# Four token-major projection blocks, first token halves shared between two engines, and a new start and end in a one-core transformer kernel

## The chip, the core and the metric

The kernel runs on one core of a Trainium2 chip. The core has a matrix engine (PE, with its weight load PEld), a vector engine (DVE), a scalar engine (ACT), GpSimd (POOL) and SyncE (SP), which here issues transfers. Data lie in SBUF, 128 partitions wide; PE writes to PSUM, whose banks hold 128 x 512 fp32 values. The metric is the device time of one execution in microseconds.

## The reference

The input is x, 256 tokens by 2048 features, with a memory of 256 rows. Two layers of one model (a pooling layer and a layer of compressed, selected and windowed attention, each with memory attention) are followed by a block of another: differential, stick-breaking and chunk-band attention side by side, an output projection, and a gated feed-forward part with a causal convolution, then a last norm. Cut to the lines that the change bears on:

```python
h = rmsnorm_2(x, attn_norm[l])
qkv = jnp.einsum('bsd,de->bse', h, w_qkv[l])
q_a, k_a, v_a, q_b, k_b, v_b, q_c, k_c, v_c = split_columns(qkv)
y_b = stick_breaking_attention(q_b, k_b, v_b, sb_norm[l])
y_c = chunk_band_attention(q_c, k_c, v_c, rel_bias[l], ch_norm[l])
...
x = x + jnp.einsum('bsf,fd->bsd', jax.nn.silu(g) * u, w_down[l])
return rmsnorm_2(x, final_norm)
```

In the program q_c, k_c, v_c are called qc, kcc, vcc, and q_b, k_b, v_b are qb, kb, vb; each is 512 wide, with eight heads of 64.

## The kernel before, in words

All weights pass through the core once, as 691 units of at most 128 x 1024 fp32 (512 KB), in the order of a plan. SP asks for a unit into one of four stage buffers `s_stage`. ACT copies it, rounded, into the high part of one of three buffers `s_w` (L1214), DVE subtracts that from the original and writes the low part (L1855), and PE multiplies high by high, high by low and low by high. The two steps are called the split. A buffer of `s_w` comes free when PE has finished the unit three before.

Each engine's program is written out by hand as one list. Its beat is the unit: `nxt` on ACT and DVE first gives every attached piece of side work one tick, then splits the next unit; on PE the tick comes after a unit's matmuls. `later(n, ...)` attaches work n ticks on. Engines meet by semaphores, and each list is worked off in order, so an instruction that waits holds what stands behind it.

A projection is done in one of two ways. Weight-stationary (`tile`, L586 and L587; `group`, L627 and L630): the weights are PE's stationary side, a unit is eight pairs of a matmul of 512 columns (the high and the low tokens) and one of 256, and the output has features on partitions and tokens in the columns. DVE then adds the two halves of the bank (L1900) and scales (L1907, L1909). Token-major (`pair`, L653 to L655): the tokens are stationary, a unit is twelve matmuls of 512 columns, and the output has tokens on partitions, one bank for each half of the 256 tokens. In the last unit of eight the first token half is finished first. DVE moves the first half out (L1922), ACT the second (L1244), with the row norm's factor. Only two banks, psg0 and psg1, serve all of this before the feed-forward part; they are taken in turn, and a first matmul into a bank waits until its last content is out.

The blocks of the feed-forward part are token-major with turned weights: ACT moves both halves to `s_ev` (L1611), and DVE transposes 32 x 32 blocks in four ticks of four instructions (`turn`, L2389), after which features lie on partitions again. They alternate between two pairs of banks.

The middle's order is qc, kcc, vcc, qb, kb, vb, all from the normalised second block's input `s_ry`. Side work there: the scaling of X by the final gain of the first model (L2306), and from the end of vcc on the chunk-band attention, four pairs of heads, six ticks apart: scores on PE (L978, L979), bias and maxima on DVE (L2324, L2325, L2047, L2048), exponentials on ACT (L1522), and the finish of a head (L2315, L2332).

At the start the memory's 256 rows come in pieces, are split with their gain (L1226 on ACT, L1873 on DVE) into `s_rh`, and the first units, of memory keys, go four tiles abreast over two column blocks of 128 features per unit. The first unit comes on ACT's queue in two halves (L1271, L1964). The squares for the memory's row norm are taken by ACT from a second copy (L1291), in bursts of four.

At the end, the last down-projection block leaves its last three units' second token half to the end; then for each token half come an addition (L2580), squares (L1652), a sum (L2584), logarithm and exponential (L1827, L1829), three refinements (L2588 to L2592), the scaling of four blocks of 512 on DVE and ACT (L2596, L2599, L1662), and four stores of 256 KB (L2957).

## Time and profile before

| | |
|---|---|
| median of 3 runs | 2006.98 us (2006.02 to 2007.39) |
| profiled execution | 2005.24 us, span 2003.4 us |
| PE busy | 1987.2 us, 99% of the span |
| DVE, ACT, POOL busy | 1499.9, 1065.5, 400.8 us |
| mean granted clock of PE | 0.999 |
| moved by the transfers | 374.80 MB, mean 187 GB/s |

A profile's times are those of one execution. A matmul's row gives its start and a duration that includes the pipeline, so the pace of PE is read from start to start, and durations of neighbours overlap. In brackets at the end of a row stands how long the engine was idle before it, and which engine, tile and line released it. DVE's next instruction may likewise start about 0.1 us before the end given for the last one.

### The profile page before, as it was taken

How to read it: one execution, taken by the hardware profiler on the slowest of the kernel's cores; microseconds unless marked ns; L12 is line 12 of the kernel's file. 1: busy time of each engine (PE TensorE's matmuls, PEld its weight loads, DVE VectorE, ACT ScalarE, POOL GpSimd, SP SyncE). 2: the span in 40 equal slices, each digit the busy share in tenths (PEclk: the TensorE clock that was granted, in tenths of full speed). 3: DMA queues.
4: the chain of work that ended last, by engine and by line, in shares of the span. 5: the costliest groups of instructions: out<-in, count | busy, mean ns of one | idle time of the engine just before them, and what ended most of it. 6: DMA issues, size and time to landing. Idle time of an engine off the chain costs nothing.

```text
span 2003.4 us, 27138 instructions
## 1 busy us (share of the span) xinstructions
PE 1987.2 (99%) x10380; PEld 1696.5 (85%) x10380; DVE 1499.9 (75%) x2180; ACT 1065.5 (53%) x1619; POOL 400.8 (20%) x379
## 2 busy tenths in 40 slices
PE   8999999999999999999999999999999999999998
PEld 7888988888888888888888888888888888888886
DVE  6776778788798666877656678688899545989954
ACT  6654544467534554654555555455555444555544
POOL 0014544300000444420222235200000100000120
PEclk9999999999999999999999999999999999999999
DMA  9664666567655334556444445655655655555564
GB/s 341 226 192 150 192 187 198 190 210 238 221 172 169 126 116 137 186 204 196 161 159 157 148 157 190 206 184 185 199 189 192 203 191 187 194 195 190 191 206 150
DMA packets 103795, 374.80 MB, mean 187 GB/s; under 512 B 11729, under 2 KB 13169, under 8 KB 103153
## 3 DMA queue, kind: packets, MB, share of 16 engines
q1 hardware_dynamic: 103376, 372.54, 56.8%
q8 instruction: 82, 1.34, 0.3%
q10 hardware_dynamic: 288, 0.52, 0.1%
q14 instruction: 49, 0.39, 0.1%
HBM read 370.92 MB, written 2.10 MB: 186 GB/s over the span
## 4 chain that ended last, share of the span: by engine, by line
PE 98%; DVE 1%; DMA 0%; ACT 0%; issue 0%; SPq 0%; ACTq 0%
PE psg L586 27%; PE psg L587 14%; PE psg L653 7%; PE psg L654 7%; PE psg L655 7%; PE pss L653 4%; PE pss L654 4%; PE pss L655 4%; PE pst L683 2%; PE pss L683 2%; PE pss L685 2%; PE pss L684 2%; PE pst L685 2%; PE pst L684 2%; PE psg L627 1%; PE pst L627 1%
## 5 line engine op out<-in xcount | busy, mean ns | idle before, releaser
L1855 DVE TENSOR_TENSOR s_w<-s_stage,s_w 128x1024 fp32r<-128x1024 f32 (+2 forms) x690 | 855.6, 1242 | 314.7 <-ACT s_w L1214 310.5
L1214 ACT ACTIVATE s_w<-s_stage 128x1024 fp32r<-128x1024 f32 (+2 forms) x690 | 725.5, 1053 | 667.0 <-PE psg L587 313.2
L586 PE MATMUL psg<-s_ry,s_w 128*128 128x512 f32 x1216 | 429.4, 394 | 0.2 <-DVE s_w L1855 0.2
L586 PE MATMUL psg<-s_rh,s_w 128*128 128x512 f32 x1216 | 427.6, 394 | 0.3 <-DVE s_w L1855 0.3
L587 PE MATMUL psg<-s_rh,s_w 128*128 128x256 f32 x1216 | 342.7, 282 | 0.0
L587 PE MATMUL psg<-s_ry,s_w 128*128 128x256 f32 x1216 | 342.6, 282 | 0.0
L586 PEld LDWEIGHTS psg<-s_ry,s_w 128*128 128x128 f32 x1216 | 228.3, 188 | 51.3 <-issue 4.1
L586 PEld LDWEIGHTS psg<-s_rh,s_w 128*128 128x128 f32 x1216 | 228.3, 188 | 48.9 <-issue 1.0
L587 PEld LDWEIGHTS psg<-s_rh,s_w 128*128 128x128 f32 x1216 | 229.8, 189 | 0.6
L587 PEld LDWEIGHTS psg<-s_ry,s_w 128*128 128x128 f32 x1216 | 229.8, 189 | 0.2
L653 PE MATMUL psg<-s_w,s_ry 128*128 128x512 f32 x512 | 201.2, 393 | 0.0
L655 PE MATMUL psg<-s_w,s_ry 128*128 128x512 f32 x512 | 199.4, 389 | 0.0
L654 PE MATMUL psg<-s_w,s_ry 128*128 128x512 f32 x512 | 199.4, 389 | 0.0
L2782 POOL TENSOR_TENSOR s_hid<-s_hh,s_hid 128x256 fp32r<-128x256 f32 x44 | 51.0, 1160 | 584.1 <-ACT s_hid L1637 584.1
L653 PE MATMUL pss<-s_w,s_ry 128*128 128x512 f32 x352 | 137.4, 390 | 0.0
L655 PE MATMUL pss<-s_w,s_ry 128*128 128x512 f32 x352 | 137.0, 389 | 0.0
L654 PE MATMUL pss<-s_w,s_ry 128*128 128x512 f32 x352 | 136.9, 389 | 0.0
L653 PEld LDWEIGHTS psg<-s_w,s_ry 128*128 128x128 f32 x512 | 96.1, 188 | 21.2 <-issue 0.8
L655 PEld LDWEIGHTS psg<-s_w,s_ry 128*128 128x128 f32 x512 | 96.1, 188 | 20.4
L654 PEld LDWEIGHTS psg<-s_w,s_ry 128*128 128x128 f32 x512 | 96.2, 188 | 19.2
L2650 POOL TENSOR_SCALAR s_bsc<-s_bsc,s_stat 128x256 f32<-128x256 f32 (+1 forms) x56 | 45.8, 836 | 184.7 <-DVE s_stat L2289 173.5
L2389 DVE STREAM_TRANSPOSE s_gg<-s_ev 32x256 f32<-32x256 f32 x176 | 76.7, 436 | 2.8
(424 smaller groups left out, 2973.9 us busy)
## 6 DMA issues: line engine op xcount, KB each, us to landing
s_stage<-in_wo SPq DMA_DIRECT2D x96, 512.0 KB, 3.5
s_stage<-in_wg SPq DMA_DIRECT2D x88, 512.0 KB, 3.3
s_stage<-in_wu SPq DMA_DIRECT2D x88, 512.0 KB, 3.3
s_stage<-in_wd SPq DMA_DIRECT2D x88, 512.0 KB, 3.4
s_stage<-in_ain SPq DMA_DIRECT2D x64, 512.0 KB, 3.7
s_stage<-in_wkv SPq DMA_DIRECT2D x32, 512.0 KB, 3.4
s_stage<-in_bq SPq DMA_DIRECT2D x24, 512.0 KB, 3.4
s_stage<-in_bzq SPq DMA_DIRECT2D x24, 512.0 KB, 3.2
```

Source lines behind the costliest of these rows:

```text
L586: e.matmul(o, M.WH[:, r, ws], xx, start=begin, stop=False)
L587: m = e.matmul(o[:, T:2 * T], M.WL[:, r, ws], xh, start=False, stop=end)
L653: e.matmul(o[:, :], xh[:, ts], M.WH[:, r, ws], start=(k == 0), stop=False)
L654: e.matmul(o[:, :], xh[:, ts], M.WL[:, r, ws], start=False, stop=False)
L655: m = e.matmul(o[:, :], xl[:, ts], M.WH[:, r, ws], start=False, stop=(k == 15))
L683: e.matmul(o, xh[:, ts], M.WH[:, r, ws], start=(k == 0), stop=False)
L684: e.matmul(o, xh[:, ts], M.WL[:, r, ws], start=False, stop=False)
L685: m = e.matmul(o, xl[:, ts], M.WH[:, r, ws], start=False, stop=(k == nk - 1))
L1214: e.activation(M.weights(c, 0, n, shift), M.staged(c, n), ACT.Copy).then_inc(S["wh"], 1)
L1855: e.tensor_tensor(M.weights(c, 1, n, shift), M.staged(c, n), M.weights(c, 0, n, shift), ALU.subtract).then_inc(S["wl"], 1)
L2389: x = e.transpose(dst[32 * r:32 * r + 32, :, :].rearrange("p c (t q i) -> p q t c i", t=2, q=4)[:, q, :, :, :], M.EV[32 * q:32 * q + 32, r ...
L2782: e.tensor_tensor(M.HID[:, 1, i, :], M.HH[j % 2][:, :], M.HID[:, 0, i, :].bitcast(F32), ALU.subtract).then_inc(S["hidl"], 1)
```

## The change

It has three parts.

Start: eleven matmuls of 128 columns on the constant tile `s_one` are issued by PE before its first unit. The second unit is asked for in two halves, ahead of memory pieces 2 and 3, and is split in halves. The first unit's matmuls are issued with the four tiles' high products first, then the low ones. Memory pieces 4 to 7 come in two transfers, the vector of constants later, and the squares of the memory's rows in bursts of two.

Middle: qc, kcc, qb and kb become token-major blocks with turned weights. ACT moves both token halves of qc and the second one of the three others into `s_ev2` (shown as `s_ev`); DVE moves the first half of kcc, qb and kb, with `first_half`, which stands in its list behind the split of the second unit after the block. Four turns follow in the ticks of the next block. The chunk-band and stick-breaking scores wait for the turns. The scaling of X begins 14 ticks later.

End: the second token half of the last three units is done in two halves of 256 columns, the second of them in a bank of its own; the sums of three of the four blocks' squares are taken ahead, the fourth enters through the logarithm's bias; DVE, ACT and POOL share the scaling; each token half is stored in two transfers of 512 KB.

Some semaphores of the constants' transfers are merged. The diff, cut to its core:

```diff
--- before.py
+++ after.py
-MEMP = ((0, 1), (1, 2), (2, 4), (4, 8), (8, 12), (12, 16))
+MEMP = ((0, 1), (1, 2), (2, 4), (4, 6), (6, 8), (8, 12), (12, 16))
...
-    P.group([("qc", j) for j in range(4)], "qc")
-    for j in range(4):
-        P.tile(("kcc", j), P.halves("kc", j))
+    P.block("qc", "qc")
+    P.block("kcc", "kc", first="out")
     P.pair("vcc", "vc")
-    for n in ("qb", "kb"):
-        for j in range(4):
-            P.tile((n, j), P.halves(n, j))
+    P.block("qb", "qb", first="out")
+    P.block("kb", "kb", first="out")
     P.pair("vb", "vb")
...
+    def first_unit(tiles, x, ready):
+        for t in tiles:
+            held[P.bank[t]] = P.out[t]
+        for k in range(2):
+            xh, xx, _ = x(k)
+            ready(k)
+            w.wait_ge(("wh_a", "wh")[k], 1)
+            for n in range(4):
+                ws = slice(512 * k + 128 * n, 512 * k + 128 * n + 128)
+                e.matmul(M.product(P.bank[tiles[n]])[:, :], M.WH[:, 0, ws], xx, start=k == 0, stop=False)
+            w.wait_ge(("wl_a", "wl")[k], 1)
+            for n in range(4):
+                ws = slice(512 * k + 128 * n, 512 * k + 128 * n + 128)
+                m = e.matmul(M.product(P.bank[tiles[n]])[:, T:2 * T], M.WL[:, 0, ws], xh, start=False, stop=False)
+        m.then_inc(S["units"], 1)
...
+        def last_columns(c):
+            for h in range(2):
+                if h:
+                    vacant(("s", 0))
+                o = last_bank(M) if h else down_bank(M, 3, 1)[:, 0:256]
+                for u in range(nk // 2 - 3, nk // 2):
+                    r = (c + u - nk // 2 + 3) % NR
+                    for kk in range(2):
+                        k = 2 * u + kk
+                        xh, _, xl = x(k)
+                        ws = slice(SHIFT + 512 * kk + 256 * h, SHIFT + 512 * kk + 256 * h + 256)
+                        e.matmul(o, xh[:, 128:256], M.WH[:, r, ws], start=h == 1 and k == nk - 6, stop=False)
+                        e.matmul(o, xh[:, 128:256], M.WL[:, r, ws], start=False, stop=False)
+                        m = e.matmul(o, xl[:, 128:256], M.WH[:, r, ws], start=False, stop=k == nk - 1)
...
     def ch_pair(p):
         vacant(("s", 0), ("s", 1))
-        w.wait_ge(*P.out["kcc", 3])
-        w.wait_ge(*P.out["qc", 3])
+        w.wait_ge("turned", P.turned["kcc"] + 4)
...
+    w.wait_ge("eps", 1)
+    for n in range(11):
+        e.matmul(M.PSO[0][:, 0:128], ones, ones, start=True, stop=True)
...
+    def evacuate(tile, ev, rc, n):
+        w.wait_ge("nr_dve", 3 * NORM[n] + 3)
+        if P.turned[tile]:
+            w.wait_ge("turned", P.turned[tile])
+        for t in range(P.out[tile, 0][0] == "out", 2):
+            if t:
+                w.wait_ge("units", P.end[tile, 1])
+            else:
+                w.wait_ge("half", P.half[tile])
+            src = M.product(P.bank[tile, t]).rearrange("p (r f) -> p r f", r=4)
+            e.activation(ev[:, :, t, :], src, ACT.Copy, scale=rc[:, t:t + 1]).then_inc(S["out_act"], 1)
...
-                if q == 3 or i and q == 1:
+                if q % 2:
                     yield
...
+    def first_half(tile, ev, rc, scale):
+        w.wait_ge("half", P.half[tile])
+        w.wait_ge("turned", P.turned[tile])
+        src = M.product(P.bank[tile, 0]).rearrange("p (r f) -> p r f", r=4)
+        e.tensor_scalar(ev[:, :, 0, :], src, rc[:, 0:1], scale, ALU.mult, ALU.mult).then_inc(S["out"], 1)
...
-    nxt(3)
+    nxt(5)
     normed("eff")
-    for j in range(4):
-        scaled(("qc", j), M.QC[:, j, :], 0.125, 1)
-        if j % 2:
-            nxt()
-    tiles("kcc", 4, M.KCC, None, 1)
+    side.start(turns("qc", M.QC, M.EV2))
+    nxt(7)
+    first_half("kcc", M.EV2, M.RC[1], 1.0)
+    nxt()
+    side.start(turns("kcc", M.KCC, M.EV2))
     v_pair("vcc", M.VCC[:, 0, :], 1, "eff_c")
     for p in range(4):
         side.start(later(6 * p, ch_pair(p)))
-    tiles("qb", 4, M.QB, 0.125, 1)
-    tiles("kb", 4, M.KB, None, 1)
+    nxt(7)
+    first_half("qb", M.EV2, M.RC[1], 0.125)
+    nxt()
+    side.start(turns("qb", M.QB, M.EV2))
+    nxt(7)
+    first_half("kb", M.EV2, M.RC[1], 1.0)
+    nxt()
+    side.start(turns("kb", M.KB, M.EV2))
     v_pair("vb", M.VB[:, 0, :], 1, "eff_c", 1)
...
-    for n in range(3):
-        memory(n)
+    memory(0)
+    memory(1)
+    for half, name in enumerate(("st_b", "st1")):
+        ws = slice(512 * half, 512 * half + 512)
+        e.dma_start(M.ST[:, 1, ws], P.units[1][0][:, ws]).then_inc(S[name], 16)
+        issued[0] = 2
+    memory(2)
     weights()
     memory(3)
     weights()
...
-    for t in range(2):
-        for n, name, i in ((3, "f_dve", 6 * t + 5), (0, "f_act", 4 * t + 3), (2, "f_dve", 6 * t + 6), (1, "f_act", 4 * t + 4)):
-            w.wait_ge(name, i)
-            e.dma_start(out[t, :, block(n)], M.OT[:, t, block(n)]).then_inc(S["stored"], 16)
-    w.wait_ge("stored", 128)
+    def store(t, a, b):
+        e.dma_start(out[t, :, a:b], M.OT[:, t, a:b]).then_inc(S["stored"], 16)
```

The queue of transfers on SP at the program's start (`s_mem` the memory's pieces, `s_stage` the units, of which the first is asked for by ACT), before:

```order
L2920 DMA s_vec<-in_vec 128x16
L2914 DMA s_mem<-in_mem 128x256 x2
L2914 DMA s_mem<-in_mem 128x512
L2910 DMA s_stage<-in_mk0 128x1024
L2914 DMA s_mem<-in_mem 128x1024
L2910 DMA s_stage<-in_mk0 128x1024
```

and now:

```order
L3057 DMA s_vec<-in_vec 128x16
L3051 DMA s_mem<-in_mem 128x256 x2
L3062 DMA s_stage<-in_mk0 128x512 x2
L3051 DMA s_mem<-in_mem 128x512
L3047 DMA s_stage<-in_mk0 128x1024
L3051 DMA s_mem<-in_mem 128x512
```

Unit 1 has moved, in two halves, ahead of memory pieces 2 and 3.

DVE's list around the end of qb (splits write `s_w`; `s_csc`, `s_stat` and `s_yt` belong to the chunk-band attention, `s_rb` and `s_rc` are norm factors), before:

```order
L2324 TENSOR_TENSOR s_csc<-pss,s_bt 128x2x128
L2325 TENSOR_TENSOR s_csc<-pss,s_bt 128x2x256
L2047 TENSOR_REDUCE s_stat<-s_csc 128x2
L2048 TENSOR_REDUCE s_stat<-s_csc 128x2
L1855 TENSOR_TENSOR s_w<-s_stage,s_w 128x1024
L1900 TENSOR_REDUCE s_qb<-psg 128x256
L1909 SCALAR_TENSOR_TENSOR s_qb<-s_qb,s_rb 128x256
L1855 TENSOR_TENSOR s_w<-s_stage,s_w 128x1024
L2315 SCALAR_TENSOR_TENSOR s_yt<-pso,s_vec,s_et 128x256
L2332 RECIPROCAL s_stat<-s_stat 128x4
L1855 TENSOR_TENSOR s_w<-s_stage,s_w 128x1024
```

and now:

```order
L2138 TENSOR_REDUCE s_stat<-s_csc 128x2
L2139 TENSOR_REDUCE s_stat<-s_csc 128x2
L1927 TENSOR_TENSOR s_w<-s_stage,s_w 128x1024
L2018 TENSOR_SCALAR s_ev<-psg,s_rc 128x4x128
L2399 SCALAR_TENSOR_TENSOR s_x<-s_x,s_vec,s_rb 128x256
L1927 TENSOR_TENSOR s_w<-s_stage,s_w 128x1024
L2399 SCALAR_TENSOR_TENSOR s_x<-s_x,s_vec,s_rb 128x256
L2408 SCALAR_TENSOR_TENSOR s_yt<-pso,s_vec,s_et 128x256
L2425 RECIPROCAL s_stat<-s_stat 128x4
L2024 STREAM_TRANSPOSE s_qb<-s_ev 32x2x4x32 x4
L1927 TENSOR_TENSOR s_w<-s_stage,s_w 128x1024
L2399 SCALAR_TENSOR_TENSOR s_x<-s_x,s_vec,s_rb 128x256
```

Where the reduction and the scaling of a qb tile stood, the eviction of the whole block's first token half stands, behind the same split; the turns come in the ticks after it, beside the later scaling of X.

DVE's list for the second token half at the end, before:

```order
L2580 TENSOR_TENSOR s_ot<-pst,s_ot 128x512
L2584 TENSOR_REDUCE s_fs<-s_ss 128x1
L2588 SCALAR_TENSOR_TENSOR s_fw<-s_fs,s_fr 128x1
L2590 SCALAR_TENSOR_TENSOR s_fw<-s_fw,s_fr 128x1
L2592 SCALAR_TENSOR_TENSOR s_fr<-s_fw,s_fr 128x1
L2596 SCALAR_TENSOR_TENSOR s_ot<-s_ot,s_fr,s_fg 128x512
L2599 TENSOR_SCALAR s_ot<-s_ot,s_fr 128x512
```

and now:

```order
L2695 SCALAR_TENSOR_TENSOR s_fb<-s_ss,s_fb 128x1
L2696 TENSOR_TENSOR s_fs<-s_fs,s_ss 128x1
L2680 TENSOR_TENSOR s_ot<-pss,s_ot 128x256
L2701 SCALAR_TENSOR_TENSOR s_fw<-s_ss,s_fs,s_fr 128x1
L2703 SCALAR_TENSOR_TENSOR s_fw<-s_fw,s_fr 128x1
L2705 SCALAR_TENSOR_TENSOR s_fr<-s_fw,s_fr 128x1
L2721 TENSOR_SCALAR s_ot<-s_ot,s_fr 128x512
L2711 SCALAR_TENSOR_TENSOR s_ot<-s_ot,s_fr,s_fg 128x256
L2725 TENSOR_SCALAR s_ot<-s_ot,s_fr 128x256
```

The last addition is half as wide, and the reduction has left the place between it and the refinements.

## Rows read from the trace of the kernel before

**Rows 1.** The page: chain that ended last, share of the span by engine.

```profile
PE 98%; DVE 1%; DMA 0%; ACT 0%; issue 0%; SPq 0%; ACTq 0%
```

**Rows 2.** By windows: span, busy us (count) by engine, clock, DMA share, GB/s.

```profile
5.80:9.30 3.50, 3.44 (x10) 2.72 (x11) 2.51 (x5) 2.24 (x5) 0.00 (x0) 1.00 0.94 349
...
12.10:20.00 7.90, 7.90 (x48) 7.00 (x47) 5.95 (x9) 5.99 (x11) 0.00 (x0) 1.00 1.01 399
```

**Rows 3.** Timeline, PE, first units: start us, duration us, operation, [idle, releaser].

```profile
5.86 0.77 PE L627 MATMUL psg<-s_rh,s_w 128*128 128x512 f32 x1 [5.86 <-DVE s_rh L1873]
...
11.16 0.50 PE L627 MATMUL psg<-s_rh,s_w 128*128 128x512 f32 x1 [0.51 <-DVE s_w L1855]
...
14.04 0.39 PE L627 MATMUL psg<-s_rh,s_w 128*128 128x512 f32 x1
```

**Rows 4.** Timeline, ACT and DVE, 7 to 11 us.

```profile
7.52 0.91 ACT L1226 ACTIVATE s_rh<-s_mem,s_vec 128x256 fp32r<-128x256 f32 x2 [0.89 <-DMA s_mem<-in_mem]
...
8.79 1.06 ACT L1214 ACTIVATE s_w<-s_stage 128x1024 fp32r<-128x1024 f32 x1 [0.37 <-DMA s_stage<-in_mk]
...
8.06 0.88 DVE L1873 SCALAR_TENSOR_TENSOR s_rh<-s_mem,s_vec,s_rh 128x256 fp32r<-128x256 f32 x2 [0.63 <-ACT s_rh L1226]
...
9.88 1.23 DVE L1855 TENSOR_TENSOR s_w<-s_stage,s_w 128x1024 fp32r<-128x1024 f32 x1 [0.94 <-ACT s_w L1214]
```

**Rows 5.** Timeline, PE, two matmuls on s_one (four records) and what follows.

```profile
52.72 0.61 PE L754 MATMUL pso<-s_nw,s_one 128*128 128x128 f32 x4
...
53.08 0.48 PE L627 MATMUL pst<-s_ry,s_w 128*128 128x512 f32 x1
```

**Rows 6.** Timeline, PE, first matmuls of units 12 and 14, token-major.

```profile
41.57 0.39 PE L653 MATMUL psg<-s_w,s_rh 128*128 128x512 f32 x1
...
47.28 0.39 PE L653 MATMUL psg<-s_w,s_rh 128*128 128x512 f32 x1
```

**Rows 7.** Timeline, PE, first matmuls of weight-stationary units, four units apart.

```profile
901.44 0.39 PE L586 MATMUL psg<-s_ry,s_w 128*128 128x512 f32 x1
...
912.53 0.39 PE L586 MATMUL psg<-s_ry,s_w 128*128 128x512 f32 x1
```

**Rows 8.** Timeline, PE, first matmuls of token-major units, five units apart.

```profile
920.95 0.39 PE L653 MATMUL psg<-s_w,s_ry 128*128 128x512 f32 x1
...
934.54 0.39 PE L653 MATMUL psg<-s_w,s_ry 128*128 128x512 f32 x1
```

**Rows 9.** Timeline, DVE and PE, the boundary from vs to vw.

```profile
514.38 0.74 DVE L1922 TENSOR_SCALAR s_vs<-psg,s_rc 128x512 f32<-128x512 f32 x1
...
515.18 0.50 PE L653 MATMUL psg<-s_w,s_rh 128*128 128x512 f32 x1 [0.58 <-DVE s_vs L1922]
```

**Rows 10.** Timeline, PE and DVE, the boundaries of qb, kb and vb.

```profile
963.50 0.39 PE L586 MATMUL psg<-s_ry,s_w 128*128 128x512 f32 x1
...
963.86 0.68 DVE L1900 TENSOR_REDUCE s_qb<-psg 128x256 f32<-128x512 f32 x1
...
987.24 1.32 DVE L1855 TENSOR_TENSOR s_w<-s_stage,s_w 128x1024 fp32r<-128x1024 f32 x1 [0.22 <-ACT s_w L1214]
...
988.66 0.40 PE L653 MATMUL psg<-s_w,s_ry 128*128 128x512 f32 x1
```

**Rows 11.** Timeline, DVE, one turn of a feed-forward block.

```profile
1410.62 1.78 DVE L2389 STREAM_TRANSPOSE s_uu<-s_ev 32x256 f32<-32x256 f32 x4
```

**Rows 12.** By windows, PE: fifteen steps of 256-column matmuls in the pool layer.

```profile
201.15:202.90 1.75, 1.75 (x17) 1.75 (x16) 1.45 (x4) 1.36 (x2) 0.00 (x0) 1.00 0.80 185
```

**Rows 13.** Timeline, PE, ACT and DVE, the end.

```profile
1994.32 0.39 PE L685 MATMUL pst<-s_w,s_hid 128*128 128x512 f32 x1
...
1995.47 0.63 ACT L1652 ACTIVATE s_jk<-s_ot 128x512 f32<-128x512 f32 x1 [0.66 <-DVE s_ot L2580]
...
1997.56 0.75 DVE L2596 SCALAR_TENSOR_TENSOR s_ot<-s_ot,s_fr,s_fg 128x512 f32<-128x512 f32 x1
```

**Rows 14.** DMA traffic in 40 slices of 0.25 us from 1994 us on.

```profile
GB/s 0 0 0 0 197 377 393 377 401 377 385 385 377 369 385 172 0 0 0 0 90 385 385 393 360 393 369 401 377 369 393 262 25 25 0 0 0 0 0 0
```

More of the change, by code:

```diff
@@ L245, in residual, with block @@
             self.tile((name, j), units(j))
-    def block(self, m):
-        tile = ("ff", m)
+    def block(self, tile, name, b=0, banks=None, first="out_act"):
+        self.turned[tile] = len(self.turned) * 4
         for t in range(2):
-            self.bank[tile, t] = ("sg"[m % 2], t)
+            if banks:
+                self.bank[tile, t] = (banks, t)
+            else:
+                self.take((tile, t))
         for u in range(8):
-            self.unit(self.A[("wg", "wu")[m % 2]][8 * (m // 2) + u], 1024, SHIFT)
+            self.unit(self.A[name][8 * b + u], 1024, SHIFT)
             if u == 7:
                 self.half[tile] = len(self.half) + 1
-                self.close((tile, 0), "out_act")
+                self.close((tile, 0), first)
                 self.close((tile, 1), "out_act")
@@ L702, in down @@
                 products(n, u, (c + u - apart) % NR, [(0, 0), (1, 0)])
-            for u in range(apart, nk // 2):
-                products(n, u, (c + u - apart) % NR, [(0, 1), (1, 1)]).then_inc(S["units"], 1)
-                unit()
+            if apart < nk // 2:
+                last_columns(c)
     def flips():
@@ L1165, in eff_hook @@
         side.start(eff_norms())
-    group([("qc", j) for j in range(4)], Y, ready("hc"), eff_hook)
-    for j in range(4):
-        tile(("kcc", j), Y, ready("hc"))
+    pair("qc", Y, ready("hc"), eff_hook)
+    pair("kcc", Y, ready("hc"))
     pair("vcc", Y, ready("hc"))
@@ L1680, in scalar_program @@
     mem0(0)
-    first(0)
+    first(0, 0)
     mem0(1)
-    first(1)
+    first(0, 1)
+    first(1, 0)
     mem0(2)
+    first(1, 1)
     mem0(3)
@@ L1940, in silu, with turn, turns @@
         e.scalar_tensor_tensor(dst[:, :], M.ET[i % 2][:, :], 1.0, M.ZT[i % 2][:, :], ALU.add, ALU.mult).then_inc(S["z_d"], 1)
+    def first_half(tile, ev, rc, scale):
[3 more added lines that the diff above has]
+        e.tensor_scalar(ev[:, :, 0, :], src, rc[:, 0:1], scale, ALU.mult, ALU.mult).then_inc(S["out"], 1)
+    def turn(tile, q, dst, ev):
+        w.wait_ge(*P.out[tile, 0])
+        w.wait_ge(*P.out[tile, 1])
+        for r in range(4):
+            x = e.transpose(dst[32 * r:32 * r + 32, :, :].rearrange("p c (t q i) -> p q t c i", t=2, q=4)[:, q, :, :, :],
+                            ev[32 * q:32 * q + 32, r, :, :].rearrange("p t (c i) -> p t c i", c=4))
+        x.then_inc(S["turned"], 1)
+    def turns(tile, dst, ev):
+        for q in range(4):
+            turn(tile, q, dst, ev)
+            yield
     def gate(rb, *t):
@@ L2303, in eff_norms @@
         w.wait_ge("sqc2", KT)
+        for _ in range(14):
+            yield
         for j in range(KT):
@@ L2395, in gate_block @@
             w.wait_ge("ff_v", 2 * (2 * m))
-        for q in range(4):
-            turn(m, q, M.GG)
-            yield
+        yield from turns(("ff", m), M.GG, M.EV)
         for c in range(4):
@@ L2410, in up_block @@
             w.wait_ge("ff_h", 2 * m - 2)
-        for q in range(4):
-            turn(m, q, M.UU)
-            yield
-        w.wait_ge("turned", 4 * m + 4)
+        yield from turns(("ff", m), M.UU, M.EV)
+        w.wait_ge("turned", P.turned["ff", m] + 4)
         for c in range(4):
```

267 lines of the change are left out of this document (172 added, 95 removed).

## The prediction

> **What bounds the kernel now.** I read the page's chain of waits first, then the start by windows and timeline, then the block boundaries of the middle, then the tail. The chain is PE for 98% of the span [rows 1], so a term counts only where it shortens or lengthens PE's own run, or the few microseconds after its last matmul. The profiled execution took 2005.24 us (span 2003.4); the three runs shown have their median at 2006.98, 1.74 higher. The sum below is made against the profiled one and the shift is applied to the median.
>
> The reader is to see three things. At the start ten matmuls take 3.5 us, though the granted clock of the stretch is recorded as 1.00, and later 48 take 7.9 [rows 2]. PE begins unit 0 at 5.86, then sits idle 0.51 before unit 1 at 11.16, waiting for DVE's low part of it; unit 2 begins at 14.04 [rows 3]. Behind that wait stands the queue of transfers: memory pieces 2 and 3 reach ACT at 7.52, and ACT's split of unit 1, which waited for its weights, starts at 8.79 and DVE's at 9.88 [rows 4].
>
> **The start.** Unit 1 is now asked for, in two halves, before memory piece 2. The bytes in front of the later of the two are the same, so piece 2 lands where unit 1 did, just before 8.79, and unit 1 about 0.6 and 1.3 us earlier. Unit 1 then waits for the token-norm parts: ACT's high part of column block 2 takes 0.91/2 = 0.46 and DVE's low part 0.88/2 = 0.44 [rows 4], so PE may start block 2 at about 8.8 + 0.46 + 0.44 + two handovers of 0.05 = 9.8. A unit lasts 2.773, four of them 912.53 - 901.44 [rows 7], so unit 1 ends near 12.6. Unit 2 follows its transfer at about 10.1: ACT 1.06, DVE 1.23, then DVE's low part of block 4, 0.44, which stands behind the split: 12.85. That is 14.04 - 12.85 = 1.19 earlier than now.
>
> Does unit 0 end in time? Eleven warm-up matmuls on `s_one` run before it. Two such matmuls take four records and 53.08 - 52.72 = 0.36 us of PE [rows 5], so eleven take 2.0 us at full speed and 4.0 at half. PE has nothing else before 5.86 [rows 3]; begun in the first microsecond they end by 5.0. With the clock up, unit 0 takes 2.8 and ends at 8.6, and the memory block decides. With it down at first, as now, unit 0, which ends at 11.16 - 0.51 = 10.65, ends at about 10.2, since the small gaps of its first pairs go, and unit 2 begins at 10.2 + 2.77 = 12.97. So the warm-up itself is worth 0.12 at this place, and I keep 1.19. The first ten matmuls at half pace under a recorded clock of 1.00 [rows 2] speak for a chip that starts at 1.2 GHz and rises with use. The Trainium skill ("TensorE: Matmul & The Clock Gate", Part 1, What's actually happening) says so: throttled by default, released by activity, and the record of it is not to be trusted; by that rule unit 0 ends at 8.6, without it at 10.2, and the sum changes by the 0.12 just named.
>
> Second, the squares of the memory rows go from bursts of four to bursts of two on ACT. Two units there took 47.28 - 41.57 = 5.71 [rows 6] where two of token-major work take 2 x 2.718 (five in 934.54 - 920.95, [rows 8]): 0.27 of stall that I expect to go. The start is thus -1.46. Bounds: -0.5, if block 2 lands late and the stall stays, and -2.4, if unit 2 is not held by DVE either and follows unit 0 directly.
>
> **The middle.** Thirty-two units (qc, kcc, qb, kb) change from 2.773 [rows 7] to 2.718 [rows 8]: 32 x 0.055 = -1.7. Their reductions and scalings on DVE go, and 16 turns of four transposes come. A token-major block needs both psg banks, and so does the next one, whose first matmul waits until the first token half is out. For qc that eviction is ACT's, ahead of its other work, and is done before the block ends. For kcc, qb and kb it is DVE's, and stands behind DVE's split of the unit two after the block's last; queued behind it on DVE are the turns and the later splits, which have a unit's length of lead.
>
> The boundary from vs to vw has the same order: the eviction began at 514.38, took 0.74, and PE stood 0.58 waiting for it [rows 9]; the first matmul after a stall lasts 0.50 against 0.39 [rows 3, 9], another 0.11. That gives:
> - kcc to vcc, with no other DVE work in the tick: 0.58 + 0.11 = 0.69.
> - qb to kb: DVE's chunk-band bias and maxima precede the split, and DVE is free at 963.86, where now it reduces a qb tile, while PE could start kb at 963.50 [rows 10]. Eviction until 964.60 and a handover of 0.06: 1.16 + 0.11 = 1.27.
> - kb to vb: the split starts at 987.24 and has its follower about 1.24 later, so the eviction ends at 989.22; PE could start vb at 988.66 [rows 10]: 0.62 + 0.11 = 0.73.
>
> Together +2.69, and the middle +0.99. What is hidden: the second token half is ACT's and is wanted only six matmuls into the next block, 1.36 us. The delayed scaling of X costs nothing while PE has 2.7 us per unit. Bounds: -1.7 if no boundary waits, +2.5 if kb and vb wait for a late low part as well.
>
> A row speaks on moving evictions to DVE: it takes 0.74 for a bank of 512 [rows 9], so the engine itself costs little; its place behind a split is what costs. The Trainium skill ("VectorE: DVE Perf Modes", Why PSUM operands drop a tier) says that an fp32 source in PSUM leaves VectorE at its single rate, which agrees with 0.74, and ("Advanced Engine Details and Errata", The Read-Write Bubble) that ScalarE is the engine nearer to PSUM; by that rule all three first halves belong on ACT, and the 2.69 would be saved. Both agree that the three evictions are a loss.
>
> **The end.** The last three units' second token half is done in two 256-column halves. Steps of 256 columns take 1.75/15 = 0.117 [rows 12], so 36 of them take 4.21, against 18 of 2.718/12 = 0.2265, 4.08: PE ends 0.12 later. After it, now: last matmul 1994.32 (+0.39), add, square from 1995.47, reduction, logarithm, exponential, three refinements, scaling from 1997.56 [rows 13]. From the square to the scaling is 2.09. With 256 columns square and add lose about 0.25 each, and the reduction with its handovers (0.19 to 0.2) leaves the chain, while an eviction in between on DVE gives some 0.15 back: 0.12 - 0.25 - 0.25 - 0.19 + 0.15 = -0.42 at the scaling; I take -0.41. The stores move 1 MB: at the full rate of about 385 GB/s 2.72 us, but now the last burst spans 3.25 us, from slice 20 to the end of slice 32 [rows 14], since four issues feed it. Two of 512 KB should close most of the gaps: -0.37. The end is -0.78. Bounds: 0 (the split columns cost what they give) and -1.3.
>
> **Sum.** -1.46 + 0.99 - 0.78 = -1.25: 2003.99 for an execution like the profiled one, 2005.7 at the median. The measurement of this kernel tells apart about 0.2%, 4 us, so the forecast is no change that can be told.
>
> **Rivals.**
> 1. *The boundaries do not wait* (0.15). For it: DVE loses 32 operations of reduction and scaling, so its splits could run earlier than the rows show. Against: the split ahead of each eviction waits for a weight buffer that a unit of PE frees, not for DVE, and vs to vw waits in just this state [rows 9]. Time: -1.46 - 1.7 - 0.78 = -3.94, 2003.0.
> 2. *The start gives nothing* (0.17): block 2's parts come later than unit 1's did, since they share ACT with the half splits. For it: ACT would do a half split (about half of 1.06) between them. Against: there is a gap of 0.37 before 8.79 [rows 4]. Only the 0.27 and a little more stay: -0.4, total -0.2, 2006.8.
> 3. *The end gives nothing* (0.10): the two column halves and DVE's other work there use up what was saved. Total -0.47, 2006.5.
> 4. *DVE's queue falls behind in the turned blocks, and the kernel is slower* (0.08). A tick of DVE in kb holds a turn, 1.78 in the feed-forward blocks [rows 11], a scaling of X, 0.44 like the low parts, and a split, about 1.14 to its follower: 3.36 against 2.72 of PE. The four ticks lose 2.6 us, of which the lead of one unit (2.7 at most) covers nearly all. So it decides from turns just over 1.8 on. If the transposes into s_qb and s_kb, which no row shows, took half as long again (2.67), four ticks in each of four blocks would lose 16 x 0.89 = 14.2, less a lead of about 1.6 left in three of them and 2.7 in one, 7.5: +6.7, and the total would be +5.4, 2012.4. Against: the same form and size of transpose runs in the feed-forward blocks, and the tile's layout is theirs.
>
> The forecast has the rest, 0.50, with its own range from 2004.5 to 2007.2, half from the three bounds and half from the spread of single runs.
>
> **How the numbers follow.** Faster by over 0.2% means below 2003.0: half of rival 1 and the far end of the start's bound, 0.07 + 0.05 = 0.12. Slower means above 2011.0: most of rival 4, 0.05. The rest, 0.83, is no change. The range that should hold the time 8 times in 10 goes from 2003.0 (rival 1) to 2007.8 (rivals 2 and 3 with 1 us on top), and leaves out rival 4 and the far ends.
>
> **What would show it.** Right: unit 2 starts near 12.85 and unit 0 ends before 9; no stall near 44; PE idles of about 0.6, 1.2 and 0.6 before vcc, kb and vb, released by DVE's writes of s_ev; none before kcc; token-major steps of 0.227 throughout; the last scaling some 2.3 us after the last matmul's end. Wrong: PE waiting at ticks within kb or vb for the low part (rival 4), or no idle at the three boundaries (rival 1), or unit 1 still at 11 (rival 2).

## The result: 0.17% slower

The changed kernel takes 2009.6 us (median of 21 runs, 2008.55 to 2012.98), the kernel before 2006.4 in the same sessions (21 runs, 2005.25 to 2007.72). The ratio is 1.0017, with a 95% interval from 1.0011 to 1.0023: slower by 2.2 to 4.6 us, where 1.25 us less, 2005.7, were forecast. The profiled execution took 2009.15, with a span of 2007.3, 3.9 longer than before.

### The profile page after: what moved, and what is told of

It reads as the page before. It is cut to its first block, busy times and chain, and to the rows that moved or that the text cites. A ratio compares the mean times of both kernels' runs of the same rounds, so it can differ in the third digit from the quotient of the medians.

```text
span 2007.3 us, 27021 instructions
## 1 busy us (share of the span) xinstructions
PE 1990.1 (99%) x10292; PEld 1692.9 (84%) x10292; DVE 1515.9 (76%) x2223; ACT 1068.9 (53%) x1628; POOL 409.0 (20%) x381
## 4 chain that ended last, share of the span: by engine, by line
PE 94%; DVE 3%; ACT 1%; POOL 1%; issue 1%; DMA 1%; SPq 0%; ACTq 0%; DVEq 0%
PE psg L596 25%; PE psg L597 13%; PE psg L681 7%; PE psg L683 7%; PE psg L682 7%; PE pss L681 4%; PE pss L682 4%; PE pss L683 4%; PE pss L712 2%; PE pss L711 2%; PE pss L713 2%; PE pst L711 2%; PE pst L712 2%; PE pst L713 2%; PE psg L657 1%; DVE s_w L1927 1%
## 5 line engine op out<-in xcount | busy, mean ns | idle before, releaser
L1927 DVE TENSOR_TENSOR s_w<-s_stage,s_w 128x1024 fp32r<-128x1024 f32 x689 | 854.4, 1242 | 309.7 <-ACT s_w L1260 304.5
L1260 ACT ACTIVATE s_w<-s_stage 128x1024 fp32r<-128x1024 f32 x689 | 724.1, 1053 | 656.5 <-PE psg L597 288.6
L596 PE MATMUL psg<-s_ry,s_w 128*128 128x512 f32 x1024 | 361.6, 394 | 0.2 <-DVE s_w L1927 0.2
L597 PE MATMUL psg<-s_ry,s_w 128*128 128x256 f32 x1024 | 288.4, 282 | 0.0
L681 PE MATMUL psg<-s_w,s_ry 128*128 128x512 f32 x640 | 252.5, 395 | 3.3 <-DVE s_ev L2018 3.3
L683 PE MATMUL psg<-s_w,s_ry 128*128 128x512 f32 x640 | 249.3, 390 | 0.0
L682 PE MATMUL psg<-s_w,s_ry 128*128 128x512 f32 x640 | 249.3, 390 | 0.0
L596 PEld LDWEIGHTS psg<-s_ry,s_w 128*128 128x128 f32 x1024 | 192.3, 188 | 42.5 <-issue 3.1
L597 PEld LDWEIGHTS psg<-s_ry,s_w 128*128 128x128 f32 x1024 | 193.5, 189 | 0.1
L681 PEld LDWEIGHTS psg<-s_w,s_ry 128*128 128x128 f32 x640 | 120.1, 188 | 31.7 <-DVE s_ev L2018 4.6
L683 PEld LDWEIGHTS psg<-s_w,s_ry 128*128 128x128 f32 x640 | 120.1, 188 | 25.5
L682 PEld LDWEIGHTS psg<-s_w,s_ry 128*128 128x128 f32 x640 | 120.2, 188 | 24.0
```

What stands on the lines that cost most here:

```text
L596: e.matmul(o, M.WH[:, r, ws], xx, start=begin, stop=False)
L597: m = e.matmul(o[:, T:2 * T], M.WL[:, r, ws], xh, start=False, stop=end)
L681: e.matmul(o[:, :], xh[:, ts], M.WH[:, r, ws], start=(k == 0), stop=False)
L682: e.matmul(o[:, :], xh[:, ts], M.WL[:, r, ws], start=False, stop=False)
L683: m = e.matmul(o[:, :], xl[:, ts], M.WH[:, r, ws], start=False, stop=(k == 15))
L1260: e.activation(M.weights(c, 0, n, shift), M.staged(c, n), ACT.Copy).then_inc(S["wh"], 1)
```

## The profile after

Where the time went is read from the same points of PE's program in both profiles. The timeline of PE in the changed kernel, at the first matmul of unit 14, qc, vcc, kb and vb, at the last pair's product with vcc in the chunk-band attention, which PE does one unit into va (this point is called va below), and at the last matmul:

```profile
45.78 0.39 PE L681 MATMUL psg<-s_w,s_rh 128*128 128x512 f32 x1
...
867.65 0.40 PE L681 MATMUL psg<-s_w,s_ry 128*128 128x512 f32 x1
...
914.11 0.50 PE L681 MATMUL psg<-s_w,s_ry 128*128 128x512 f32 x1 [0.42 <-DVE s_ev L2018]
...
963.90 0.50 PE L681 MATMUL psg<-s_w,s_ry 128*128 128x512 f32 x1 [1.03 <-DVE s_ev L2018]
...
991.88 0.50 PE L681 MATMUL psg<-s_w,s_ry 128*128 128x512 f32 x1 [1.88 <-DVE s_ev L2018]
...
1021.77 0.44 PE L1047 MATMUL pso<-s_cpt,s_vcc 128*64 128x256 f32 x2
...
1999.37 0.28 PE L731 MATMUL pss<-s_w,s_hid 128*128 128x256 f32 x1
```

The kernel before, for the two points that no group above shows (qc and va; start us, duration us, operation):

```profile
868.66 0.39 PE L627 MATMUL pst<-s_ry,s_w 128*128 128x512 f32 x1
...
1017.21 0.66 PE L1001 MATMUL pso<-s_cpt,s_vcc 128*64 128x256 f32 x4
```

Against [rows 6, 10, 13] and these two, the changed kernel's PE is 1.50 us ahead at unit 14, 1.01 ahead at qc, 0.40 behind at kb, 3.22 behind at vb, 4.56 behind at va and 5.05 behind at the last matmul; the span ends 3.9 later. So the start gave 1.50, the middle lost 5.57, and from va on 0.66 came back. From unit 14 to qc 0.49 was lost in between; PE's wait at the boundary from vs to vw [rows 9], whose code is the same, is 0.64 longer there.

PE's waits in the changed kernel (what waited, for what; us in total, times, longest):

```profile
PE psg L681 <- DVE s_ev L2018: 3.3, 3, 1.9
PE pst L1035 <- POOL s_csc L2780: 2.0, 4, 0.7
PE psg L681 <- DVE s_vs L1994: 1.2, 1, 1.2
```

The first line is the three evictions by DVE. The second is new: PE's transposes of the chunk-band attention's probabilities wait for POOL, in all four pairs; before, no row of PE's waits named POOL there. The third is the boundary from vs to vw, 0.58 before.

The start, PE's timeline: the warm-up (22 records), unit 0, unit 1, unit 2.

```profile
0.97 4.14 PE L1136 MATMUL pso<-s_one 128*128 128x128 f32 x22 [0.97 <-POOL s_eps L2928]
5.91 0.70 PE L622 MATMUL psg<-s_rh,s_w 128*128 128x512 f32 x2 [0.79 <-ACT s_w L1329]
...
9.63 0.50 PE L657 MATMUL psg<-s_rh,s_w 128*128 128x512 f32 x1 [0.69 <-DVE s_rh L1945]
...
12.73 0.47 PE L657 MATMUL psg<-s_rh,s_w 128*128 128x512 f32 x1
```

The warm-up is over by 5.1 and unit 0 lasts 3.0 us, until 8.95. Unit 1 waits 0.69 for a memory block's low part, as worked out, and unit 2 begins at 12.73 where 12.85 was expected [rows 3].

The chunk-band attention's first pair, before: POOL's normalisation, four operations of which the first is named, and the first of PE's transposes of its result.

```profile
947.50 4.08 POOL L2650 TENSOR_SCALAR s_csc<-s_csc,s_stat 128x128 f32<-128x128 f32 x4 [62.13 <-DVE s_stat L2332]
...
952.20 0.82 PE L989 MATMUL pst<-s_cons,s_csc 128*128 128x128 f32 x6
```

and in the changed kernel:

```profile
946.59 4.78 POOL L2780 TENSOR_SCALAR s_csc<-s_csc,s_stat 128x128 f32<-128x128 f32 x4 [60.17 <-DVE s_stat L2425]
...
951.43 0.87 PE L1035 MATMUL pst<-s_cons,s_csc 128*128 128x128 f32 x6 [0.55 <-POOL s_csc L2780]
```

Before, POOL ended at 951.58 and PE came at 952.20: 0.62 of lead. PE runs about 1.3 us earlier in the changed kernel here, but POOL starts only 0.91 earlier and takes 0.70 longer, so PE waits 0.55. The reason for the longer normalisation shows in single operations: in the changed kernel the first and second of POOL's four, with the one of DVE beside them, and the fourth; then, of the kernel before, the second.

```profile
946.59 1.66 POOL L2780 TENSOR_SCALAR s_csc<-s_csc,s_stat 128x128 f32<-128x128 f32 x1 [60.17 <-DVE s_stat L2425]
...
946.64 1.22 DVE L1927 TENSOR_TENSOR s_w<-s_stage,s_w 128x1024 fp32r<-128x1024 f32 x1
...
948.25 0.60 POOL L2780 TENSOR_SCALAR s_csc<-s_csc,s_stat 128x128 f32<-128x128 f32 x1
...
949.74 1.64 POOL L2780 TENSOR_SCALAR s_csc<-s_csc,s_stat 128x256 f32<-128x256 f32 x1
```

```profile
948.09 1.61 POOL L2650 TENSOR_SCALAR s_csc<-s_csc,s_stat 128x128 f32<-128x128 f32 x1
```

The same scaling of 128 x 128 takes 1.66 us while DVE subtracts a weight's two parts, and 0.60 alone; one of 128 x 256 takes 1.64, and 0.92 alone. In these rows POOL is held while DVE runs a split, an operation with two sources in SBUF. The Trainium skill ("SBUF — State Buffer", SBUF: two separate sides) states it: GpSimd and VectorE share a pair of ports that one of them holds for a whole instruction, and VectorE claims it with two SBUF inputs; the 1.66 against 0.60 agrees, though POOL's row begins 0.05 before DVE's. Before, one of the four operations ran beside a split (1.61); now two do, which makes the 0.70. The scaling of X, which now runs here, has two sources too, but holds POOL little: in e9 a scaling of 128 x 256 beside it and one more such operation took 1.17.

The other pairs are late for other reasons. From the first matmul of a pair's scores to the end of POOL's normalisation it was 11.43, 11.46, 11.47 and 12.53 us before; now it is 12.53, 14.04, 14.30 and 15.50. The leads, from POOL's end to PE's coming, were 0.62, 0.61, 0.73 and 2.07. In the second pair POOL is no slower (3.62, before 3.72), and most of the loss stands on ACT. ACT's timeline, the first exponential before, and in the changed kernel the move of qb's second token half and the first exponential:

```profile
962.84 0.40 ACT L1522 ACTIVATE s_csc<-s_csc,s_stat 128x128 f32<-128x128 f32 x1 [1.29 <-DVE s_stat L2048]
```

```profile
962.98 0.69 ACT L1308 ACTIVATE s_ev<-psg,s_rcs 128x512 f32<-128x512 f32 x1 [2.99 <-PE psg L683]
...
964.38 0.39 ACT L1580 ACTIVATE s_csc<-s_csc,s_stat 128x128 f32<-128x128 f32 x1
```

The move waits for the block's last matmul and stands ahead of the exponentials, which so begin 5.39 us after the scores instead of 3.09. In the third pair DVE's bias comes 1.72 later, as shown next, and POOL takes 1.13 longer. In the fourth, two turns of kb stand on DVE ahead of the reciprocal, which comes 2.04 later, and POOL takes 0.92 longer.

The stretch ahead of vb, DVE's timeline: the last turn of qb, a split, the third pair's bias, and further on its reciprocal, the split before the eviction, and the eviction.

```profile
980.44 1.79 DVE L2024 STREAM_TRANSPOSE s_qb<-s_ev 32x256 f32<-32x256 f32 x4
982.26 1.23 DVE L1927 TENSOR_TENSOR s_w<-s_stage,s_w 128x1024 fp32r<-128x1024 f32 x1
983.40 0.42 DVE L2417 TENSOR_TENSOR s_csc<-pss,s_bt 128x256 f32<-128x256 f32 x1
...
989.89 0.17 DVE L2425 RECIPROCAL s_stat<-s_stat 128x4 f32<-128x4 f32 x1
989.97 1.20 DVE L1927 TENSOR_TENSOR s_w<-s_stage,s_w 128x1024 fp32r<-128x1024 f32 x1
991.08 0.75 DVE L2018 TENSOR_SCALAR s_ev<-psg,s_rc 128x512 f32<-128x512 f32 x1
```

Before, the bias began 1.33 us after DVE had run dry, as soon as the scores were there. Now the scores wait behind the turn and a split, the exponentials behind the bias, ACT's splits behind the exponentials, and the eviction that vb needs ends at 991.83, not at the 989.22 of the forecast. From 967.22 to the bias DVE has had no pause: each of qb's four ticks holds a split, a scaling of X and a turn. Without X (e1) the bias begins 0.99 after the scores, as before, and PE's wait ahead of vb is 0.42.

The end, DVE's last addition and first scaling, and ACT's last square:

```profile
2000.01 0.41 DVE L2680 TENSOR_TENSOR s_ot<-pss,s_ot 128x256 f32<-128x256 f32 x1
...
2002.26 0.49 DVE L2721 TENSOR_SCALAR s_ot<-s_ot,s_fr 128x512 f32<-128x512 f32 x1
...
2000.46 0.42 ACT L1704 ACTIVATE s_jk<-s_ot 128x256 f32<-128x256 f32 x1 [0.35 <-DVE s_ot L2680]
```

and the traffic of the transfers in 40 slices of 0.25 us from 1998 us on:

```profile
GB/s 0 0 0 0 0 0 0 0 0 115 393 393 393 442 360 213 410 377 410 393 279 49 0 279 442 377 426 426 377 410 393 442 344 279 0 0 0 0 0 0
```

From PE's last matmul to the scaling it is 2002.26 - 1999.37 = 2.89, where it was 3.24 [rows 13]. The last burst of stores lies within slices 23 to 33, where it had taken slices 20 to 33, the last two at 25 GB/s [rows 14].

## The experiments

Theory A: the loss is side work. The scaling of X, moved beside the chunk-band attention, and the turns delay the chain from the scores to PE's transposes on DVE, and POOL's part of it is slowed; the evictions suffer from the same queue. Theory B: the loss is the three DVE evictions, which stand behind splits whatever else is there. Each kernel was timed with the kernel before on the same chip (8 to 11 runs); differences below are of the medians. A ratio's interval reaches about 1.8 us to either side, so smaller differences rest on "middle", which is read from one profiled execution of each kernel: the shift of PE from qc to va, read as above, +5.57 in the changed kernel, 0 in the one before.

**X at its old place** (e1), the rest as changed:

```diff
         w.wait_ge("sqc2", KT)
-        for _ in range(14):
-            yield
```

> The changed kernel with the scaling of X begun 14 ticks earlier, as before. Theory A (the loss is side work: the later scaling of X stands on DVE ahead of the chunk-band chain and inside the turned ticks of kb, and slows POOL's normalisation): PE's waits for POOL's s_csc fall from 2.0 us to under 1.0, the wait before vb from 1.9 to about 0.7, and the time falls by 2 to 3 us, to about 2007. Theory B (the three DVE evictions stand behind DVE's splits, whatever else is in the list): the three waits for s_ev stay at 3.3 us and the time within 0.7 us of the changed kernel. A cost that either may add: the turns of qc and kcc now share their ticks with X, up to 1 us.

Measured 2007.2, +1.15 (ratio 1.0004, 0.9995 to 1.0013): 2 us of the 3.2 are gone. Middle +3.44. PE's waits:

```profile
PE psg L681 <- DVE s_ev L2018: 1.9, 3, 1.0
...
PE pst L1035 <- POOL s_csc L2778: 0.8, 2, 0.5
...
PE psg L681 <- DVE s_w L1927: 0.4, 1, 0.4
```

The evictions wait 1.9 in all where it was 3.3, with the same code: B falls as the whole cause. The last line is the price of X and turns in one tick. The profiled execution took 2009.5, the longest of the eleven, for a reason outside the middle: PE waited 1.78 at the boundary from vs to vw, and then the granted clock fell (PE's timeline, then by windows):

```profile
515.18 0.50 PE L681 MATMUL psg<-s_w,s_rh 128*128 128x512 f32 x1 [1.78 <-DVE s_vs L1994]
```

```profile
516.20:519.40 3.20, 3.20 (x9) 2.41 (x9) 1.05 (x2) 0.00 (x0) 0.00 (x0) 0.50 0.52 174
```

The unit takes 4.82 there, where it takes 3.26 in the kernel before.

**All first halves by ACT** (e2):

```diff
-    P.block("kcc", "kc", first="out")
+    P.block("kcc", "kc")
...
-    nxt(7)
-    first_half("kcc", M.EV2, M.RC[1], 1.0)
-    nxt()
+    nxt(8)
```

and likewise for qb and kb.

> The changed kernel with ACT moving both token halves of all four blocks. Theory B (evictions): the three waits for s_ev, 3.3 us and 0.3 of restarts, go, and the time falls by 3 to 3.6 us to about 2006. Theory A (side work): the waits before vcc and kb go (1.5 us with restarts), that before vb turns partly into a wait for the low part of a weight, POOL's 2.0 us stay, and the time falls by 1.5 to 2.5 us, to about 2007.5.

Measured 2009.52, +3.47 (1.0017, 1.0008 to 1.0026): no gain in the median, which neither theory had said. Middle +4.71, 0.86 better than the changed kernel, but in the fastest of the eleven executions (2007.68); why the median shows none of it is open. In the middle PE waits for one thing only:

```profile
PE pst L1035 <- POOL s_csc L2774: 4.7, 4, 2.1
```

The waits at the boundaries went, and the waits for POOL grew from 2.0 to 4.7. PE had been held at the boundaries, and that had hidden how late the chain was. ACT's two moves of a block still stand ahead of the second pair's exponentials.

**Both** (e3), the two diffs above together.

> Both edits together. Theory A: the two gains add up nearly, 4 to 5.5 us, to about 2004.5. Theory B: no more than the evictions alone, about 2006.

Measured 2006.47, +0.42 (1.0002, 0.9994 to 1.0011); middle +2.62. The second edit gives 0.7 in the medians once X is out of the way and nothing before, 0.8 and 0.9 in the middle, so the gains don't add up as A had it (2004.5); B's 2006 is near, but the evictions alone, its reason, gave nothing in the median.

**The old middle** with the new start and end (e4):

```diff
-    P.block("qc", "qc")
-    P.block("kcc", "kc", first="out")
+    P.group([("qc", j) for j in range(4)], "qc")
+    for j in range(4):
+        P.tile(("kcc", j), P.halves("kc", j))
```

with the code of before for all four blocks.

> The middle of the kernel before, with the new start and the new end. Trace reading: start -1.5, end -0.75, so 2004.2 against 2006.4 before; if the later landing of a weight at the boundary from vs to vw, 0.6 us in the changed kernel's profile, comes with the new start, 2004.8. Rival theory C (the new start or end costs more than the profile shows, the middle less): above 2006.

Measured 2004.12, -1.93 (0.9992, 0.9983 to 1.0000); middle +0.06. The two ends give what was forecast for them, -2.24, within the spread, and the middle alone costs the changed kernel some 5 us. The profiled execution was one of the slower ones (2006.32): PE waited 1.79 from vs to vw, and the clock fell as in e1; the middle lies behind that.

**The old middle with the late X** (e9):

```diff
         w.wait_ge("sqc2", KT)
+        for _ in range(14):
+            yield
```

> The old middle with new start and end, but the scaling of X begun 14 ticks later, so that it lies beside the first two chunk-band pairs; no turns, no evictions. Theory A1 (the later X alone delays the chunk-band chain): PE waits for s_csc at the first pair or two, 0.4 to 1.4 us in all, and the time is 2004.5 to 2005.5. Theory A2 (it takes the turns as well): no wait for s_csc, 2004.1 like the old middle.

Measured 2004.58, -1.16 (0.9995, 0.9986 to 1.0004); middle +1.13, all of it in one wait:

```profile
PE pst L1038 <- POOL s_csc L2769: 0.9, 1, 0.9
```

So the late X costs by itself, without a turn or an eviction. In the medians it is 0.8 more than in e4, inside the intervals.

**The normalisation on DVE** (e5), with the rest as changed:

```diff
         e.reciprocal(sv[:, 12:16], sv[:, 8:12]).then_inc(S["l2_rc"], 1)
+        w.wait_ge("l2_rc", p + 1)
+        for t, (a, b) in enumerate(CSEG):
+            for i in range(2):
+                x = e.tensor_scalar(sc[:, i, a:b], sc[:, i, a:b], sv[:, 12 + 2 * t + i:13 + 2 * t + i], None, ALU.mult)
+        x.then_inc(S["l2_nm"], 1)
```

and POOL's `normalize` of these pairs left out.

> The changed kernel with the chunk-band attention's normalisation (four scalings by the reciprocal) done by DVE right after the reciprocal, not by POOL. Theory A (the chunk-band chain comes late: X and the turns ahead of it on DVE, then POOL slowed while DVE runs an operation with two SBUF sources): PE's waits for s_csc, 2.0 us and 0.4 of restarts, go; DVE's list grows by about 1 us per pair, which may add up to 1 us before vb; the time falls by 1 to 2.4 us to about 2007.5. Theory B (evictions): no change, or slower by what DVE has more to do.

Measured 2012.21, +6.27 (1.0028, 1.0018 to 1.0038): slower by 3 us more, against A's expectation. The waits for POOL are gone, as it said. But the eviction before vb comes 1.37 later, PE idles 3.27 there, and then (by windows: span, busy us (count) by engine, clock, DMA share, GB/s):

```profile
985.00:989.90 4.90, 4.90 (x21) 3.49 (x19) 3.15 (x5) 3.77 (x10) 0.00 (x0) 1.00 0.59 205
989.90:993.20 3.30, 0.08 (x1) 0.00 (x0) 3.27 (x9) 1.94 (x3) 1.97 (x1) 0.87 0.51 159
993.25:998.50 5.25, 5.25 (x12) 4.01 (x13) 2.72 (x5) 0.00 (x0) 0.00 (x0) 0.50 0.62 203
```

the granted clock is 0.50, 1.2 of 2.4 GHz, for the next 5 us. PE's timeline at the same place, with the idle time in brackets:

```profile
993.25 0.79 PE L681 MATMUL psg<-s_w,s_ry 128*128 128x512 f32 x1 [3.27 <-DVE s_ev L2018]
993.84 0.63 PE L682 MATMUL psg<-s_w,s_ry 128*128 128x512 f32 x1
```

A matmul lasts 0.63 instead of 0.39 and the unit 5.3 instead of 2.7. With the transposes behind it the unit takes 6.17, where it takes 3.47 in the kernel before: the idle time cost 2.7 us more than itself. So this run shows that POOL's waits go, and not what they cost.

**All by ACT, the normalisation on DVE, X four ticks late** (e7):

```diff
-        for _ in range(14):
+        for _ in range(4):
```

with the edits of e2 and e5.

> All four blocks token-major, all evictions by ACT, normalisation by DVE, the scaling of X 4 ticks later than before. If side work was the whole loss, the middle comes near its pace gain: 2004.1 (old middle) less 1.7 to 1.9, plus what waits remain where turns share ticks with X (up to 1 us): 2002.5 to 2003.5. If the turns themselves fill DVE beside the chunk-band work, waits for low parts or late scores remain at 1 to 3 us: 2004 to 2006.

Measured 2006.08, +0.14 (1.0000, 0.9991 to 1.0008); middle +1.85. No wait for POOL, but 1.9 us of waits for low parts: DVE's ticks with a turn and X, or with a turn and the chunk-band work, are longer than a unit.

**Only qc and kcc, by ACT, X four ticks late** (e6); qb and kb as before:

```diff
-    P.block("qb", "qb", first="out")
-    P.block("kb", "kb", first="out")
+    for n in ("qb", "kb"):
+        for j in range(4):
+            P.tile((n, j), P.halves(n, j))
```

> Only qc and kcc token-major, both halves moved by ACT; qb and kb weight-stationary as before; the scaling of X begins 4 ticks later than before; new start and end. Theory A: no turns beside the chunk-band attention, so 16 units gain 0.053 each and nothing waits: 1 us under the old middle with the new start and end (2004.1), 2003.1. Rival: the scaling of X and the turns together fill DVE's ticks in vcc, up to 0.7 us of waits for low parts: 2003.8.

Measured 2003.6, -2.34 (0.9987, 0.9979 to 0.9996); middle -0.19: nearer to the rival. The wait is in vcc, where kcc's turns and X share ticks:

```profile
PE psg L682 <- DVE s_w L1926: 0.4, 1, 0.4
```

**X in ticks without a turn** (e10), the rest as changed:

```diff
-        for _ in range(14):
+        for _ in range(6):
             yield
         for j in range(KT):
...
-            yield
+            if j % 2:
+                yield
+            if j == 7:
+                for _ in range(4):
+                    yield
```

> The changed kernel with the scaling of X in the ticks of kcc and vcc that have no turn, two at a time, instead of beside qb and kb. Theory A: the wait before vb falls from 1.9 to 0.7 or less, PE's waits for s_csc to under 1 us, and no wait for low parts in kcc and vcc as in the run with X at its old place: middle about +2.6 against +5.6, 2006.5. Theory B: as the changed kernel, 2009.5.

Measured 2007.1, +1.36 (1.0006, 0.9997 to 1.0015); middle +2.57, as expected. The evictions wait 1.9 in all, as in e1, and PE waits for POOL:

```profile
PE pst L1035 <- POOL s_csc L2784: 0.8, 2, 0.5
```

**The same with all first halves by ACT** (e11).

```diff
-    P.block("qb", "qb", first="out")
-    P.block("kb", "kb", first="out")
+    P.block("qb", "qb")
+    P.block("kb", "kb")
```

on top of the diff of e10, with kcc's likewise.

> As the run before, and all first halves moved by ACT. If the waits at the boundaries were real costs: 2 us less than that run, 2004.5. If they only hid how late the chunk-band chain is: PE's waits for s_csc grow by most of what the boundaries give back, 2005.5 to 2006.5.

Measured 2004.79, -0.95 (0.9996, 0.9987 to 1.0005); middle +1.05. With X away the evictions' move gives 2.3 in the medians and 1.5 in the middle; a part comes back as waits for POOL, 1.14 in the second pair, where ACT's moves of qb stand ahead of the exponentials, and 0.55 in the fourth, behind kb's turns:

```profile
PE pst L1035 <- POOL s_csc L2778: 1.7, 2, 1.1
```

**Only qc and kcc, by ACT, X in ticks without a turn** (e12): the diffs of e6 and e10 together, with kcc's first half by ACT.

```diff
-    P.block("kcc", "kc", first="out")
+    P.block("kcc", "kc")
```

> Only qc and kcc token-major, both halves moved by ACT, X in the ticks of kcc and vcc without a turn; qb and kb weight-stationary; new start and end. The best version that the experiments point to: the 0.6 us of waits for a low part in vcc go, 16 units gain 0.053 each and the old stalls at their boundaries 0.1, so the middle is -1.0 and the time 2002.9 to 2003.2. If X two at a time is still too much for DVE's ticks: 2003.6 as with X 4 ticks later.

Measured 2002.39, -3.35 (0.9983, 0.9974 to 0.9992), the best here, faster than both kernels; middle -0.94. All PE waits left over, outside the memory's first blocks, are these:

```profile
PE psg L682 <- DVE s_vs L1993: 1.0, 1, 1.0
PE pso L1138 <- POOL s_eps L2923: 1.0, 1, 1.0
PE psg L597 <- DVE s_w L1926: 0.5, 2, 0.3
```

**No warm-up** (e8), the rest as changed:

```diff
-    w.wait_ge("eps", 1)
-    for n in range(11):
-        e.matmul(M.PSO[0][:, 0:128], ones, ones, start=True, stop=True)
```

> The changed kernel without the eleven warm-up matmuls. By the working of the forecast: unit 0 runs at half pace at first and ends near 10.2 instead of 8.7, unit 2 begins at about 13.0 instead of 12.7 to 12.9, and the time rises by 0.1 to 0.4 us, which is not to be told from none. Rival (the clock decides the start): 1 us or more.

Measured 2010.48, +4.54 (1.0022, 1.0013 to 1.0031), 1.3 more than the changed kernel with its own runs of before, against the 0.1 to 0.4 expected: its rival. The two intervals overlap; the profiles decide. PE is 0.11 behind at unit 14, where the changed kernel is 1.50 ahead. Its timeline, from unit 1 to unit 2:

```profile
11.21 0.63 PE L657 MATMUL psg<-s_rh,s_w 128*128 128x512 f32 x1
...
11.85 0.53 PE L657 MATMUL psg<-s_rh,s_w 128*128 128x512 f32 x1
...
12.34 0.39 PE L657 MATMUL pst<-s_rh,s_w 128*128 128x512 f32 x1
...
14.42 0.39 PE L657 MATMUL psg<-s_rh,s_w 128*128 128x512 f32 x1
```

The first pair's step is 0.64, the second's 0.49, and then six pairs take 2.08, 0.35 each: half pace lasts until about 12, not until 9.3. The traces' records of the clock begin at 9.47 in the kernel before, at 12.14 here and at 4.00, during the warm-up, in the changed kernel, each at 1.00; ahead of the first record the views print 1.00 too. So the 1.00 of [rows 2] for the first stretch is no recorded clock, and the warm-up had PE at full pace before unit 0.

## Why the prediction was wrong

**The step that failed** is the sentence in the middle's part that the delayed scaling of X "costs nothing while PE has 2.7 us per unit", with its neighbour that what queues behind the eviction on DVE has "a unit's length of lead". Both counted only the weights' low parts, for which there is such a lead. The list carries a second chain, from the scores over DVE, ACT, DVE and POOL to PE's transposes a fixed number of ticks later, and that had 0.62 us of lead. It was left out of the sum. In the middle, X beside it costs 1.1 without any turn (e9) and 2.1 in the changed kernel (e1); the new form of qb and kb beside it costs, net of its pace, the difference from e12 to e11, 2.4 in the medians and 2.0 in the middle. That second part touches another sentence, that the second token half is ACT's and hidden: it is for PE's next block, but ACT's move stands ahead of the second pair's exponentials and delays them by 2.30; kb's turns do the like to the fourth pair on DVE. Putting ACT's move behind the exponentials was not tried.

**The middle's other terms.** The pace, 0.055 a unit, was right where PE does nothing else: kcc gains about 0.05 a unit, but qc gives 0.28 in eight units and qb, in e11, 0.29, so the four blocks give less than 1.7. kcc to vcc shifts PE by 0.67 (0.69 forecast) and qb to kb by 1.27 (1.27). kb to vb has 2.10 instead of 0.73: the mechanism stood, but the rows of before had DVE free on time, and in the changed kernel it is not. The fourth rival, DVE's queue behind in the turned blocks, had the place (kb) and the resource right and the point wrong: I let it decide from the low parts, with turns that would have to be longer than 1.8. The turns took just 1.78, and it decided through the chunk-band chain.

**Theory B**, the evictions: as a cause of its own it is worth 2.7 by the forecast and 0 to 2.3 in the runs' medians, depending on what else is late (e2, e3, e11). The rule of the Trainium skill that put them on ScalarE ("Advanced Engine Details and Errata", The Read-Write Bubble) is borne out by e11 against e10, 2.3 us, and not by e2's median: the place in the queues decides, as forecast, and the late chain takes back what it gives.

**The start** came to -1.50 for -1.46, but for a reason that I had priced at 0.12, so that the size is right by luck. Without the warm-up the whole of it is gone (e8): with unit 1's new place and the squares in bursts of two alone, PE would be where it was. I had let half pace end at 9.3 as before; in e8 it lasted until about 12. The stall of 0.27 went as forecast: units 12 to 14 take 5.44. The warm-up with unit 1 at its old place was not run.

**The end** came to -0.80 for -0.78 (0.14 more was lost on the way from va), by errors that cancel. The last matmul starts 0.35 later where +0.12 stood: 256-column steps took 0.120 and not the 0.117 of [rows 12], which makes 0.12 of the difference, and the rest comes from comparing starts, since the last matmul is now half as wide. The scaling comes 0.35 sooner after that start, so it is no earlier than before where -0.41 stood; it comes 2.61 after the last matmul's end, not 2.3. The stores end 0.80 sooner where 0.37 stood.

**Not settled:** the boundary from vs to vw. PE waits 1.22 there in the changed kernel's profile, 0.58 before, and 0.58 to 2.43 in those of the twelve experiments, with the same code. In the changed kernel, e4 and e10, ACT's split waits there for a weight that lands late. In e1 and e4 the fall of the clock behind it costs another 1.6. With one profile of the kernel before, whether the new start makes this more frequent isn't shown; e4, e6 and e12 have it and are faster all the same.

## What to carry to other kernels

In a hand-ordered list, price a moved piece of work against every chain that passes through the engine, not only against the one that feeds the bottleneck; look for the chain with the least lead and read that lead in the trace before moving anything beside it. A wait that is taken away only helps if what comes next is on time: e2 took three away, and its median gained nothing. And a busy engine's work is best put into ticks that have room: moving X there from beside the chunk-band attention gave back 3.0 of the middle (e10), more than the 0.94 that the faster form of sixteen units brings (e12).
